# A two-layer decoder trunk on one core: gate and up projections of four small experts with separate high and low activations, and another order of the experts

## The chip, the cores and the metric

The kernel runs on one core of a Trainium2 chip. The metric is the time of one execution on the device, in microseconds (us). TensorE multiplies matrices and loads their stationary operand, VectorE (DVE), ScalarE (ACT) and GpSimd (POOL) compute elementwise, and SyncE (SP) issues the transfers of the weights.

## The reference

A sequence of 256 tokens of width 1024 goes through two layers. Layer 0 has two groups of attention heads and a dense SwiGLU. Layer 1 has stick-breaking attention and then a mixture of eight SwiGLU experts, of which the router picks two for each token. The change is in that last part:

```
def moe_swiglu(h, w_router, w_gate, w_up, w_down):
    logits = h @ w_router
    top_v, top_i = top_k(logits, 2)
    gates = sum(one_hot(top_i, 8) * softmax(top_v)[..., None])
    for e in range(8):
        y = y + gates[..., e] * ((silu(h @ w_gate[e]) * (h @ w_up[e])) @ w_down[e])
```

All numbers are float32. An expert has a gate and an up matrix of 1024 x 3584 and a down matrix of 3584 x 1024, 44 MB together, and the eight have 352 MB of the 432 MB that the kernel reads.

## The kernel before, in words

**Units.** All weights come in pieces of 128 partitions x 2048 float32 (1 MB), called units, in one fixed stream. An expert is 42 units: 14 of gate, 14 of up and 14 of down. SP (line 678) puts each into a ring of six raw slots as soon as the subtraction that used the slot six units earlier is done. The order inside an expert is written out by `moe_plan` (line 109): its 3584 hidden columns are cut into a chunk of 512 and three of 1024, and the units run gate 0 (2 units), up 0 (2), gate 1 (4), up 1 (4), down 0 (2), gate 2, up 2, down 1 (4 each), gate 3, up 3, down 2, down 3 (4 each).

**High and low parts.** The matmuls of the weights run in float32r, and the kernel splits every operand into two such parts: ACT copies a raw unit into a float32r tile `hi` (line 790, `split`), DVE subtracts it from the raw unit and writes the rest as `lo` (line 1286). Both rings have four slots in the expert stage (`HM`), and ACT fills a slot only when TensorE has used the unit four back. In program order ACT runs three units and DVE two units ahead of the step at which their other work stands (`used(k)`). The product of two split operands is made by `three` (lines 2003 to 2005): high by high, high activation by low weight, low activation by high weight, 512 columns each.

**Experts by load.** After the router, DVE sorts experts 1 to 7 by the number of their tokens (`order_experts`, line 1778). Expert 0 comes first. The four with the fewest tokens are "small" and have at most 64 tokens, or the kernel takes its other branch, which isn't taken here. The three others are "large" and have up to 128 rows. The eight places are numbered e = 0 to 7. In the kernel before, `SMALL` is [1, 3, 5, 7] and `LARGE` is [2, 4, 6], so they alternate.

**A large expert (and expert 0).** The token rows, gathered by an indirect transfer, are transposed on TensorE (`gather`, line 2467) and split into `xg_hi` and `xg_lo`. For each gate and up unit TensorE makes four groups of `three`, that is 12 matmuls (`columns`, line 2498). ACT applies Silu to the gate sums (`silu`, line 1089), DVE multiplies them with the up sums (`multiply`, line 1755), TensorE transposes the hidden activations in seven blocks of 512 columns (`g_transpose_h`, line 2560), ACT and DVE split each block (lines 1126 and 1798), and the down units take 12 matmuls each (`down`, line 2529).

**A small expert.** The 64 rows of high and the 64 rows of low activations stand side by side as one stationary operand of 128 columns, and `both` (line 2493) multiplies it by the high and by the low weights: eight matmuls for a unit, in gate, up and down. Rows 0 to 63 of the sum are then the high part's share and rows 64 to 127 the low part's. Silu isn't linear, so the two halves must be added before it. That is `turn` (line 2563): ACT copies the gate sums and the up sums out (`keep_gate`, line 1098, `keep_up`, line 1106), TensorE multiplies them by `fold64` (two identity matrices of 64 below each other) in float32, which transposes and adds the halves in one step. Then ACT applies Silu to a block of 128 x 256 (`turned_silu`, line 1114), DVE multiplies (`turned_multiply`, line 1761), and ACT and DVE split into high and low again (`turned_high`, line 1119, `turned_low`, line 1767). There are seven turns in an expert. The down sums are linear: both halves are stored and added on their way to memory (lines 766 and 768).

**Between experts.** ACT copies the down sums to SBUF (`y_copy`, line 1079), which marks the end of an expert in the trace. While expert e runs, DVE makes the table of the next one's tokens (line 1690), TensorE and DVE turn it into row numbers (lines 2592 and 1739), POOL gathers the rows (line 761). In expert 1 DVE computes where each token's results lie (`slot_numbers`, line 1715). In expert 7 POOL gathers those results (line 774) and DVE adds them (`add_result`, line 1745).

Of the kernel before, what the change touches and what calls it, by code (L numbers as in the profile page):

```python
# [29 lines left out]
P = 128  # L30
SEQ = 256
# [42 lines left out]
SMALL = [1, 3, 5, 7]  # L74
LARGE = [2, 4, 6]
# [67 lines left out]
def build(nc, x_d, rel_bias, ev_norm_mix, ev_w_in, ev_kv_norm, ev_w_uk, ev_w_uv, ev_cmp_pos, ev_cmp_w1,  # L143
# [93 lines left out]
    with ExitStack() as ctx:  # L237
# [96 lines left out]
        fold64 = after_layer0("fold64", [P, HALF])  # L334
# [50 lines left out]
        swish, h_turned = (probT[:, t].rearrange("p h q -> p (h q)").rearrange("p (s n) -> p s n", s=2) for t in range(T))  # L385
# [102 lines left out]
        t_silu_done = sem("t_silu_done")  # L488
        t_h_done = sem("t_h_done")
# [151 lines left out]
        def small_subs(e, s):  # L641

            return NSUB * len([i for i in SMALL if i < e]) + s

        def sub_slot(s):

            return s % 2
# [131 lines left out]
        def _(act):  # L779
# [283 lines left out]
            def gathered_high(e):  # L1063

                for b in range(2):
                    act.wait_ge(gathered, 2 * e + b + 1)
                    if e in SMALL:
                        act.activation(xg_hi[:, 4 * b:4 * b + 4, 0:HALF], ps[:, 4 + b, 0:SEQ].rearrange(
                            "p (k s) -> p k s", k=4), ACT.Copy).then_inc(xg_hi_ready, 1)
                        continue  # L1070
                    act.activation(xg_hi[:, 4 * b:4 * b + 4, :], ps[:, 4 + b, :].rearrange("p (k s) -> p k s", k=4),
                                   ACT.Copy).then_inc(xg_hi_ready, 1)
# [8 lines left out]
            def silu(e, c):  # L1081
# [7 lines left out]
                act.activation(work[:, 0, 0:w], ps[:, 4:4 + w // W, :].rearrange("p a n -> p (a n)"), ACT.Silu)\  # L1089
                    .then_inc(g_silu_done, 1)  # L1090

            def keep_gate(e, c):

                w = MOE_CHUNKS[c][1]
                act.wait_ge(units_used, first_of(e) + UP_AT[c])
                act.wait_ge(g_h_done, NCH * e + c)
                act.wait_ge(g_hT_done, NSUB * e + SUBS[c][0])
                act.activation(work[:, 0, 0:w], ps[:, 4:4 + w // W, :].rearrange("p a n -> p (a n)"), ACT.Copy)\  # L1098
                    .then_inc(g_silu_done, 1)

            def keep_up(e, c):

                w = MOE_CHUNKS[c][1]
                act.wait_ge(units_used, first_of(e) + UP_AT[c] + KD * w // UNIT)
                act.wait_ge(g_hT_done, NSUB * e + SUBS[c][0])
                act.activation(work[:, 1, 0:w], ps[:, 2:2 + w // W, :].rearrange("p a n -> p (a n)"), ACT.Copy)\
                    .then_inc(g_h_done, 1)

            def turned_silu(e, s):

                act.wait_ge(g_hT_done, NSUB * e + s + 1)
                if small_subs(e, s) >= 2:
                    act.wait_ge(t_h_done, small_subs(e, s) - 1)
                act.activation(swish[:, sub_slot(s)], ps[:, 7, 0:SEQ], ACT.Silu).then_inc(t_silu_done, 1)

            def turned_high(e, s):

                act.wait_ge(t_h_done, small_subs(e, s) + 1)
                act.activation(hT_both(s)[:, :, 0:HALF],
                               h_turned[:, sub_slot(s)].rearrange("p (j q) -> p j q", q=HALF), ACT.Copy)\  # L1120
                    .then_inc(g_hT_hi_ready, 1)
# [16 lines left out]
            with act.If(fits):  # L1138
                done[0] = U_MOE + HM
                gathered_high(0)  # L1140
                for e in range(NE):
# [7 lines left out]
                    if e in SMALL:  # L1149
                        used(UP_AT[0])  # L1150
                        keep_gate(e, 0)
                        used(GATE_AT[1])
                        keep_up(e, 0)
                        used(GATE_AT[1] + 2)
                        turned_silu(e, 0)
                        used(GATE_AT[1] + 3)
                        turned_high(e, 0)
                        used(UP_AT[1])
                        keep_gate(e, 1)
                        used(DOWN_AT[0])  # L1160
                        keep_up(e, 1)
                        used(GATE_AT[2])
                        if e == NE - 1:
                            act.wait_ge(placeT_done, 1)
                            act.activation(placeT[:], ps[:, 6, 0:SEQ], ACT.Copy).then_inc(placeT_ready, 1)
                        used(GATE_AT[2] + 2)
                        turned_silu(e, 1)
                        used(GATE_AT[2] + 3)
                        turned_high(e, 1)
                        used(UP_AT[2])  # L1170
                        turned_silu(e, 2)
                        keep_gate(e, 2)
                        used(UP_AT[2] + 1)
                        turned_high(e, 2)
                        used(DOWN_AT[1])
# [1577 lines left out]
```

## Time and profile before

| | |
|---|---|
| median of 3 runs | 1433.79 us (1429.02 to 1434.1) |
| the profiled execution | 1420.63 us, span 1418.8 us |
| mean granted TensorE clock | 0.986 |
| TensorE busy | 1369.0 us, 96% of the span |
| VectorE busy | 1097.6 us, 77% |
| ScalarE busy | 940.6 us, 66% |
| read from memory | 432.20 MB, mean 310 GB/s |
| expert stage (eight experts) | about 464 to 1407 us of the span |

Times of single rows are of the profiled execution. A matmul's duration in a row holds the time until its end has drained; the next one starts earlier, so the distance between two starts is what a matmul costs in a row of them. A row of a stretch gives its bounds, its length, each engine's busy time with its instructions, the granted clock (1.00 is full speed), the share of the DMA engines' time, and GB/s. "Idle before, with releaser" is the time an engine stood still ahead of the instruction, and what ended it.

### The profile page before, as it was taken

What the parts mean: (1) busy time and instruction counts of PE and PEld (TensorE: products, weight loads), DVE (VectorE), ACT (ScalarE), POOL (GpSimd) and SP (SyncE); (2) the same over time, 40 slices, a digit from 0 to 9 for tenths busy, and PEclk for the clock granted to TensorE, in tenths of its full rate; (3) what the DMA queues carried; (4) which work ended last, traced back from release to release, by engine and by line L of the source; (5) the groups of instructions that cost most, each with busy time, mean ns of one, the idle gap of its engine ahead of it and who ended that gap; (6) DMA issues with size and microseconds to landing.
All of it is one profiled execution on the core that took longest, in us unless ns stands there. A gap on an engine that the chain in (4) does not pass through costs nothing.

```text
span 1418.8 us, 16608 instructions
## 1 busy us (share of the span) xinstructions
PE 1369.0 (96%) x6550; PEld 1143.2 (81%) x6550; DVE 1097.6 (77%) x871; ACT 940.6 (66%) x767; POOL 49.3 (3%) x51
## 2 busy tenths in 40 slices
PE   8999999999999999999999999999999999999887
PEld 7886788887988788877888878878887878888766
DVE  4786644556465988888898898798898889888796
ACT  3565534335455677777777788687777777777764
POOL 0000000000010000000000000000000000002000
PEclk9999999999999999999999999999999999999998
DMA  9744455555632899999999999999999989999993
GB/s 311 214 159 149 155 205 178 178 179 177 224 119 92 334 373 382 379 387 399 322 407 390 364 400 407 393 366 398 379 374 414 408 324 397 394 368 392 412 360 115
DMA packets 136643, 439.13 MB, mean 310 GB/s; under 512 B 11520, under 2 KB 28912, under 8 KB 120816
## 3 DMA queue, kind: packets, MB, share of 16 engines
q1 hardware_dynamic: 130688, 424.24, 80.0%
q0 software_dynamic: 3392, 12.07, 2.5%
q10 hardware_dynamic: 2480, 1.69, 0.4%
q8 instruction: 54, 0.88, 0.3%
q14 instruction: 29, 0.24, 0.0%
HBM read 432.20 MB, written 5.78 MB: 309 GB/s over the span
## 4 chain that ended last, share of the span: by engine, by line
PE 73%; DVE 17%; ACT 5%; DMA 3%; issue 3%; ACTq 0%; SPq 0%; DVEq 0%
PE ps L2003 18%; PE ps L2005 18%; PE ps L2004 18%; DVE lo L1286 12%; PE ps L2575 7%; PE ps L2495 4%; PE ps L2496 4%; ACT hi L790 2%; DMA raw<-in_od_w_gate_dram 2%; PE ps L2560 1%; DMA wr<-in_od_w_router_dram 1%; ACT work L1098 1%; DVE work L1312 0%; PE ps L2299 0%; DMA x<-in_x_dram 0%
## 5 line engine op out<-in xcount | busy, mean ns | idle before, releaser
L1286 DVE TENSOR_TENSOR lo<-raw,hi 128x2048 fp32r<-128x2048 f32 (+1 forms) x403 | 904.9, 2285 | 102.9 <-ACT hi L790 101.2
L790 ACT ACTIVATE hi<-raw 128x2048 fp32r<-128x2048 f32 (+1 forms) x403 | 766.8, 1914 | 206.4 <-PE ps L2005 157.0
L2003 PE MATMUL ps<-hi,xT_hi 128*128 128x512 f32 (+1 forms) x752 | 294.6, 392 | 7.2 <-DVE lo L1286 4.6
L2005 PE MATMUL ps<-hi,xT_lo 128*128 128x512 f32 (+1 forms) x752 | 290.0, 386 | 0.0
L2004 PE MATMUL ps<-lo,xT_hi 128*128 128x512 f32 (+1 forms) x752 | 289.7, 385 | 0.0
L2495 PE MATMUL ps<-hi,xT_hi 128*128 128x512 f32 x448 | 187.4, 418 | 12.0 <-DVE lo L1286 11.0
L2496 PE MATMUL ps<-lo,xT_hi 128*128 128x512 f32 x448 | 181.4, 405 | 0.0
L2003 PEld LDWEIGHTS ps<-hi,xT_hi 128*128 128x128 f32 x752 | 141.7, 188 | 38.3 <-issue 5.5
L2005 PEld LDWEIGHTS ps<-hi,xT_lo 128*128 128x128 f32 x752 | 141.4, 188 | 28.7
L2004 PEld LDWEIGHTS ps<-lo,xT_hi 128*128 128x128 f32 x752 | 141.6, 188 | 26.4
L2495 PEld LDWEIGHTS ps<-hi,xT_hi 128*128 128x128 f32 x448 | 88.5, 198 | 45.5 <-DVE lo L1286 19.9
L2003 PE MATMUL ps<-hi,hT_hi 128*128 128x512 f32 x296 | 116.2, 393 | 0.0
L2005 PE MATMUL ps<-hi,hT_lo 128*128 128x512 f32 x296 | 115.4, 390 | 0.0
L2004 PE MATMUL ps<-lo,hT_hi 128*128 128x512 f32 x296 | 115.3, 390 | 0.0
L2575 PEld LDWEIGHTS ps<-fold,work 128*128 128x128 f32 x448 | 106.6, 327 | 1.1
L2575 PE MATMUL ps<-fold,work 128*128 128x64 f32 x448 | 104.3, 387 | 0.0
L2496 PEld LDWEIGHTS ps<-lo,xT_hi 128*128 128x128 f32 x448 | 88.1, 197 | 17.3
L2003 PE MATMUL ps<-xT_hi,hi 128*128 128x256 f32 (+1 forms) x256 | 73.0, 285 | 1.0 <-DVE lo L1286 1.0
L2004 PE MATMUL ps<-xT_lo,hi 128*128 128x256 f32 (+1 forms) x256 | 72.4, 283 | 0.0
L2005 PE MATMUL ps<-xT_hi,lo 128*128 128x256 f32 (+1 forms) x256 | 72.4, 283 | 0.0
L2005 PEld LDWEIGHTS ps<-hi,hT_lo 128*128 128x128 f32 x296 | 55.6, 188 | 11.6
L2003 PEld LDWEIGHTS ps<-hi,hT_hi 128*128 128x128 f32 x296 | 55.7, 188 | 11.1
(327 smaller groups left out, 1223.9 us busy)
## 6 DMA issues: line engine op xcount, KB each, us to landing
raw<-in_od_w_gate_dram SPq DMA_DIRECT2D x112, 1024.0 KB, 8.4
raw<-in_od_w_up_dram SPq DMA_DIRECT2D x112, 1024.0 KB, 9.4
raw<-in_od_w_down_dram SPq DMA_DIRECT2D x112, 1024.0 KB, 8.3
raw<-in_od_w_qkv_dram SPq DMA_DIRECT2D x12, 1024.0 KB, 5.2
raw<-in_ev_w_gate_dram SPq DMA_DIRECT2D x11, 1024.0 KB, 5.2
raw<-in_ev_w_up_dram SPq DMA_DIRECT2D x11, 1024.0 KB, 5.1
raw<-in_ev_w_down_dram SPq DMA_DIRECT2D x11, 1024.0 KB, 5.1
raw<-in_ev_w_in_dram SPq DMA_DIRECT2D x4, 1024.0 KB, 11.1
```

What stands on the lines that cost most here:

```text
L790: act.activation(unit(hi, n), unit(raw, n), ACT.Copy).then_inc(hi_ready, 1)
L1098: act.activation(work[:, 0, 0:w], ps[:, 4:4 + w // W, :].rearrange("p a n -> p (a n)"), ACT.Copy)\
L1286: dve.tensor_tensor(unit(lo, n), unit(raw, n), unit(hi, n).bitcast(F32), ALU.subtract)\
L2003: pe.matmul(out, s_hi, m_hi, start=start, stop=False, skip_group_check=True)
L2004: pe.matmul(out, s_hi, m_lo, start=False, stop=False, skip_group_check=True)
L2005: return pe.matmul(out, s_lo, m_hi, start=False, stop=stop, skip_group_check=True)
L2495: pe.matmul(out, s_both, m_hi, start=start, stop=False, skip_group_check=True)
L2496: return pe.matmul(out, s_both, m_lo, start=False, stop=stop, skip_group_check=True)
L2560: ins = pe.transpose(ps[:, 7, P * j:P * j + P], work[:, 1, f + j:f + W:4], ident[:])
L2575: ins = pe.matmul(ps[:, 7, first:first + HALF], work[:, part, f + j:f + W:4], fold64[:], start=True, stop=True)
```

## The change

For small experts only the down projection keeps the joined operand (`both`). Gate and up take `three` with a stationary operand of 64 columns, and write to rows 0 to 63. Silu, multiplication and transpose then go as in a large expert, on 64 rows. `turn`, its copies, its buffers and `fold64` are gone, and each engine runs one order of steps for all experts. The places change too: expert 0, the three largest, then the four small ones.

```diff
-SMALL = [1, 3, 5, 7]
-LARGE = [2, 4, 6]
+SMALL = [4, 5, 6, 7]
+LARGE = [1, 2, 3]
...
+        def rows_of(e):
+
+            return HALF if e in SMALL else P
...
-            def keep_gate(e, c):
...
-            def keep_up(e, c):
...
-            def turned_silu(e, s):
...
-            def turned_high(e, s):
...
+                n = rows_of(e)
+                act.activation(work[0:n, 0, 0:w], ps[0:n, 4:4 + w // W, :].rearrange("p a n -> p (a n)"), ACT.Silu)\
                     .then_inc(g_silu_done, 1)
...
             def g_hT_high(e, s):
 
                 act.wait_ge(g_hT_done, NSUB * e + s + 1)
+                if e in SMALL:
+                    act.activation(hT_both(s)[:, :, 0:HALF], ps[:, 7, 0:SEQ].rearrange("p (j q) -> p j q", q=HALF),
+                                   ACT.Copy).then_inc(g_hT_hi_ready, 1)
+                    return
...
-            def turned_multiply(e, s):
...
-            def turned_low(e, s):
...
+                n = rows_of(e)
+                dve.tensor_tensor(work[0:n, 1, 0:w], work[0:n, 0, 0:w],
+                                  ps[0:n, 2:2 + w // W, :].rearrange("p a n -> p (a n)"), ALU.mult).then_inc(g_h_done, 1)
...
             def g_hT_low(e, s):
 
                 dve.wait_ge(g_hT_hi_ready, NSUB * e + s + 1)
+                if e in SMALL:
+                    dve.tensor_tensor(hT_both(s)[:, :, HALF:P], ps[:, 7, 0:SEQ].rearrange("p (j q) -> p j q", q=HALF),
+                                      hT_both(s)[:, :, 0:HALF].bitcast(F32), ALU.subtract).then_inc(g_hT_ready, 1)
+                    return
...
-                        if e in SMALL:
-                            ins = both(ps[:, bank + m, :], xg_hi[:, k, :], wh[:, kk, cols], wl[:, kk, cols], k == 0,
-                                       k == KD - 1)
-                            continue
-                        ins = three(ps[:, bank + m, :], xg_hi[:, k, :], xg_lo[:, k, :], wh[:, kk, cols],
-                                    wl[:, kk, cols], k == 0, k == KD - 1)
+                        ins = three(ps[0:tokens, bank + m, :], xg_hi[:, k, 0:tokens], xg_lo[:, k, 0:tokens],
+                                    wh[:, kk, cols], wl[:, kk, cols], k == 0, k == KD - 1)
...
+                n = rows_of(e)
                 for j in range(4):
-                    ins = pe.transpose(ps[:, 7, P * j:P * j + P], work[:, 1, f + j:f + W:4], ident[:])
-                ins.then_inc(g_hT_done, 1)
-
-            def turn(e, s, c):
...
+                    ins = pe.transpose(ps[:, 7, n * j:n * j + n], work[0:n, 1, f + j:f + W:4], ident[0:n, 0:n])
                 ins.then_inc(g_hT_done, 1)
```

`gather`, `gathered_high` and `gathered_low` get the same `rows_of(e)`, and `order_experts` writes the sorted experts in one run each instead of every second place. The separate lists of steps for small experts on TensorE, ACT and DVE are taken out.

## Rows read from the trace of the kernel before

**Rows 1.** The page's first part: busy time of each engine, share of the span, instructions.

```profile
PE 1369.0 (96%) x6550; PEld 1143.2 (81%) x6550; DVE 1097.6 (77%) x871; ACT 940.6 (66%) x767; POOL 49.3 (3%) x51
```

**Rows 2.** Timeline of ACT (start, duration us): the y copy behind expert 1, of seven.

```profile
700.79 1.03 ACT L1079 ACTIVATE work<-ps 128x1024 f32<-128x1024 f32 x1 [0.18 <-PE ps L2496]
```

**Rows 3.** Stretches, experts 1, 2, 3, 5, 7: us; busy PE, PEld, DVE, ACT, POOL; clock; DMA.

```profile
583.30:700.80 117.50, 112.75 (x461) 91.68 (x459) 100.16 (x82) 90.59 (x68) 3.35 (x2) 0.96 0.98 377
700.80:820.30 119.50, 119.39 (x545) 99.30 (x546) 106.21 (x60) 88.81 (x56) 4.24 (x3) 1.00 1.01 382
820.30:932.80 112.50, 109.50 (x460) 89.42 (x459) 97.14 (x61) 90.78 (x67) 3.38 (x2) 0.98 1.00 394
...
1052.40:1167.60 115.20, 112.40 (x460) 91.50 (x458) 97.34 (x61) 91.06 (x68) 3.38 (x2) 0.96 0.98 384
...
1287.10:1407.30 120.20, 110.33 (x450) 90.67 (x448) 99.07 (x59) 86.64 (x66) 9.32 (x5) 0.96 0.87 338
```

**Rows 4.** Timeline of TensorE: a turn in small expert 1.

```profile
685.57 0.40 PE L2496 MATMUL ps<-lo,hT_hi 128*128 128x512 f32 x1
685.81 3.72 PE L2575 MATMUL ps<-fold,work 128*128 128x64 f32 x16
689.34 0.47 PE L2495 MATMUL ps<-hi,hT_hi 128*128 128x512 f32 x1
```

**Rows 5.** Timeline of TensorE: end of large expert 4, then a 64-row transpose.

```profile
1039.49 0.39 PE L2004 MATMUL ps<-lo,hT_hi 128*128 128x512 f32 x1
1039.72 0.39 PE L2005 MATMUL ps<-hi,hT_lo 128*128 128x512 f32 x1
1040.04 0.71 PE L2458 MATMUL ps<-ident,work 64*128 64x64 f32 x8
```

**Rows 6.** Groups by line, small expert 3 (820.3 to 932.8): busy us, mean ns, idle before.

```profile
L1098 ACT ACTIVATE work<-ps 128x1024 f32<-128x1024 f32 (+1 forms) x4 | 3.6, 911 | 0.0
L1106 ACT ACTIVATE work<-ps 128x1024 f32<-128x1024 f32 (+1 forms) x4 | 3.6, 908 | 0.0
L1761 DVE TENSOR_TENSOR probT<-probT,ps 128x256 f32<-128x256 f32 x7 | 3.0, 421 | 13.0 <-ACT probT L1114 13.0
L1114 ACT ACTIVATE probT<-ps 128x256 f32<-128x256 f32 x7 | 2.7, 383 | 14.6 <-PE ps L2575 14.6
```

**Rows 7.** Groups by line, large expert 4 (932.8 to 1052.4).

```profile
L1755 DVE TENSOR_TENSOR work<-work,ps 128x1024 f32<-128x1024 f32 (+1 forms) x4 | 4.3, 1087 | 2.3 <-PE ps L2005 2.3
L1089 ACT ACTIVATE work<-ps 128x1024 f32<-128x1024 f32 (+1 forms) x4 | 3.7, 920 | 1.8 <-PE ps L2005 1.8
```

**Rows 8.** A stretch inside small expert 3, columns as in rows 3.

```profile
829.40:910.00 80.60, 78.37 (x325) 63.71 (x324) 70.48 (x44) 64.72 (x48) 2.80 (x1) 0.98 1.02 409
```

**Rows 9.** Timeline of ACT in small expert 3: splits that waited for their unit.

```profile
855.54 1.92 ACT L790 ACTIVATE hi<-raw 128x2048 fp32r<-128x2048 f32 x1 [0.63 <-DMA raw<-in_od_w_gate_dram]
858.11 1.91 ACT L790 ACTIVATE hi<-raw 128x2048 fp32r<-128x2048 f32 x1 [0.65 <-DMA raw<-in_od_w_up_dram]
```

**Rows 10.** Stretches at half clock: the first and last of ten.

```profile
598.40:601.80 3.40, 3.40 (x9) 2.72 (x10) 2.67 (x3) 2.49 (x3) 0.00 (x0) 0.50 1.05 423
1397.10:1400.60 3.50, 3.50 (x10) 2.74 (x9) 3.50 (x4) 3.04 (x3) 0.00 (x0) 0.51 0.00 0
```

**Rows 11.** Timelines of DVE and ACT in large expert 2: the down stage.

```profile
753.43 8.89 DVE L1286 TENSOR_TENSOR lo<-raw,hi 128x2048 fp32r<-128x2048 f32 x4
...
763.02 1.22 DVE L1755 TENSOR_TENSOR work<-work,ps 128x1024 f32<-128x1024 f32 x1 [0.70 <-PE ps L2005]
...
791.31 1.92 ACT L790 ACTIVATE hi<-raw 128x2048 fp32r<-128x2048 f32 x1 [0.80 <-PE ps L2005]
```

**Rows 12.** Timeline of DVE in expert 1: first and last of the slot numbers.

```profile
604.21 0.58 DVE L1719 TENSOR_SCALAR rslot<-splace 128x2 f32<-128x2 f32 x7
...
607.67 0.17 DVE L1732 CAST rslot_id<-rslot_at 128x4 uint32<-128x4 f32 x1
```

**Rows 13.** Group by line in the last expert (1287.1 to 1407.3).

```profile
L1745 DVE SCALAR_TENSOR_TENSOR x<-results,rslot_gate,x 128x1024 f32<-128x1024 f32 x4 | 5.1, 1278 | 0.0
```

More of the change, by code:

```diff
@@ L1778, in order_experts @@
             def order_experts():
-                for first, count, at_load in ((0, len(SMALL), len(LARGE)), (1, len(LARGE), 0)):
-                    ins = dve.tensor_tensor(stands_at[:, first:NE - 1:2, :],
+                for first, count, at_load in ((0, len(LARGE), 0), (len(LARGE), len(SMALL), len(LARGE))):
+                    ins = dve.tensor_tensor(stands_at[:, first:first + count, :],
                                             by_load[:, at_load:at_load + count].unsqueeze(2)
@@ L2452, in gather @@
             def gather(e):
-                if e in SMALL:
-                    pe.wait_ge(rows_landed, 16 * e)
-                    pe.wait_ge(g_silu_done, NCH * e)
-                    for k in range(KD):
-                        ins = pe.transpose(ps[:, 4 + k // 4, HALF * (k % 4):HALF * (k % 4) + HALF], rows[0:HALF, P * k:P * k + P],
-                                           ident[0:HALF, 0:HALF])
-                        if k % 4 == 3:
-                            ins.then_inc(gathered, 1)
-                    return
                 if e:
@@ L2465, in gather @@
                     pe.wait_ge(g_silu_done, NCH * e)
+                    n = rows_of(e)
                     for k in range(KD):
-                        ins = pe.transpose(ps[:, 4 + k // 4, P * (k % 4):P * (k % 4) + P], rows[:, P * k:P * k + P], ident[:])
+                        ins = pe.transpose(ps[:, 4 + k // 4, n * (k % 4):n * (k % 4) + n], rows[0:n, P * k:P * k + P],
+                                           ident[0:n, 0:n])
                         if k % 4 == 3:
@@ L2500, in columns @@
                 n = first_of(e) + base + q
+                tokens = rows_of(e)
                 w = MOE_CHUNKS[c][1]
@@ L2558, in g_transpose_h @@
                 f = W * (s - SUBS[c][0])
+                n = rows_of(e)
                 for j in range(4):
-                    ins = pe.transpose(ps[:, 7, P * j:P * j + P], work[:, 1, f + j:f + W:4], ident[:])
-                ins.then_inc(g_hT_done, 1)
-            def turn(e, s, c):
-                pe.wait_ge(g_silu_done, NCH * e + c + 1)
-                pe.wait_ge(g_h_done, NCH * e + c + 1)
-                if s:
-                    pe.wait_ge(t_h_done, small_subs(e, s))
-                else:
-                    pe.wait_ge(g_hT_ready, NSUB * e)
-                f = W * (s - SUBS[c][0])
-                for part in range(2):
-                    for j in range(4):
-                        first = SEQ * part + HALF * j
-                        ins = pe.matmul(ps[:, 7, first:first + HALF], work[:, part, f + j:f + W:4], fold64[:],
-                                        start=True, stop=True)
+                    ins = pe.transpose(ps[:, 7, n * j:n * j + n], work[0:n, 1, f + j:f + W:4], ident[0:n, 0:n])
                 ins.then_inc(g_hT_done, 1)
```

183 lines of the change are left out of this document (5 added, 178 removed).

## The prediction

> **What bounds the kernel now.** I read the page's busy times first [rows 1]: TensorE is busy in 96% of the span, but a matmul's row includes its drain, so this isn't yet 96% of its rate. Then I cut the expert stage at the y copies, one behind each expert [rows 2], and read each piece [rows 3]. All large experts take 119.5 us and TensorE is busy for 119.4 of it: they are bound by TensorE. The small ones take 117.5, 112.5, 115.2 and 120.2 us (sum 465.4), though they have a third fewer matmuls in a unit. TensorE stands still there for 3 to 10 us, DVE is busy for 97 to 100 us and ACT for 87 to 91, and the clock is 0.96 to 0.98 where the large ones have 1.00. So what does a small expert wait for?
>
> Two matmuls of 512 columns start 0.23 us apart [rows 5]; 504 of them in a large expert make 114.5 us at 0.227. A unit of 12 matmuls is 2.73 us, a unit of eight 1.82. DVE subtracts one unit every 2.22 us (four in 8.89) [rows 11] and ACT copies one in 1.91 [rows 9]. A unit arrives every 2.56 us: two ACT splits that both waited for their transfer start 2.57 us apart [rows 9], and over 80 us the DMA engines are full at 409 GB/s [rows 8], where 1.0486 MB take 2.56 us. So between turns a small expert's TensorE could go at 1.82 us a unit but gets one every 2.2 to 2.6. At a turn, TensorE alone works for 3.5 us, 685.81 to 689.34 [rows 4], while the slots fill up and ACT waits for it (14.6 us in seven turns) and DVE for ACT (13.0 us) [rows 6]. The work is uneven: TensorE is too fast in one step and too slow in the next. And the clock is at its lower level, 1.2 GHz, in ten stretches of 3.4 us [rows 10], all of them in small experts, during a turn or right behind one; no large expert has any.
>
> **TensorE's work.** Removed per small expert: seven turns of 3.55 us, 24.9 us. Added: one matmul for each of 28 units x 4 groups, 112 x 0.227 = 25.4 us, and seven blocks of four transposes. Eight 64-row transposes show 0.71 us [rows 5], so 28 take 2.5. The sum is +3 us: TensorE gets more to do, not less. Counted from below: 28 x 2.73 + 14 x 1.82 = 101.9; a large expert's other work (transposes, gather, row numbers) is 119.5 - 114.5 = 5.0, and with 64 rows I take 4.0 (bounds 3 and 5). That is 106 us, against some 103 before.
>
> The trace has no float32r matmul with 64 stationary columns and 512 moving ones. By the rows at hand its cost is 0.227 us, since the moving columns are the same; a loaded array of half the columns could save nothing in a row that streams 512. Bounds: 0.21 and 0.25 us, which is -6 or +8 us per expert. I take 0.227.
>
> **DVE.** Out go seven multiplications of 0.42 us (3.0 us [rows 6]); in come four larger ones, 4.3 us [rows 7], if 64 partitions take as long as 128 (lower bound half, 2.2). The subtraction stays at 128 x 256. 97.1 - 3.0 + 4.3 = 98.4 us busy.
>
> **ACT.** Out go the two copies (3.6 + 3.6) and Silu in blocks (2.7) [rows 6]; in comes Silu on 64 rows, 3.7 [rows 7]. 90.8 - 6.2 = 84.6 us. Neither engine's sum is the bound; the turn's chain TensorE, ACT, DVE, ACT, DVE gets shorter by two links, and its waits of 13 us on DVE mostly go.
>
> **What is late next: the down units.** Gate and up now run at TensorE's 2.73 us a unit, slower than DVE (2.22) and DMA (2.56). But a down unit is 1.82 us, and there DVE is late. Walked for down 1 (four units, t = 0 where TensorE begins them): the copy of a unit starts when TensorE has used the one four back, as the ACT row's wait on TensorE says [rows 11]. Two down units are ready at t = 0. DVE's multiplication needs the last up unit and takes 1.22, then come 2.2 per unit: the third down unit is ready at 3.4, the fourth at 5.6, the next gate unit at 7.8. TensorE wants them at 3.6, 5.5 and 7.3. It loses 0.6 us. For down 2 and 3 (eight units in a row) the same walk has DVE need 1.2 + 6 x 2.2 + 1.6 (two blocks' low parts and the gathered rows), about 16.3 beyond t = 0, where TensorE needs 14.5 + 1.6 of transposes and gather, and the ordering behind transposes adds some 2: it loses 2.2. Down 0 has two units and loses nothing. So TensorE with its waits takes 106 + 2.8 = 108.8 us.
>
> **DMA.** An expert moves 44.04 MB of weights, 0.26 MB of gathered rows and 0.52 MB of stored results: 44.8 MB, at 409 GB/s [rows 8] 109.6 us. At the mean rate of all of expert 3, 394 GB/s [rows 3], it is 113.7. These are the bounds; I take 111, nearer to the saturated stretch. So DMA becomes the bound by about 2 us. The first of the four small experts follows a large one, whose pace of 2.73 us a unit lets the six raw slots fill, so 110 for it, then 111, 111.
>
> The last one also gathers 2.1 MB of results (5.1 us of DMA) and adds them in 5.1 us of DVE, among the down units [rows 13]; part of each shows, 5 in all: 116. Together 448 against 465.4: -17.4. The seven turns' half clock, at most 1.7 us for each of ten stretches [rows 10], is inside these numbers and not counted twice.
>
> **The moved step.** With the new order expert 1 is large, and the slot numbers (604.21 to 607.84, 3.6 us of DVE [rows 12]) fall into it. A large expert's DVE is ahead of TensorE by about one unit and idle 13 us in all, so most of it is hidden; bounds 0 and 3.6, I take +1.0. The gather, stores and place tables keep their place inside an expert. Four small experts in a row instead of alternating costs only that DMA can't catch up between them, which is priced above. At the end, the same steps follow the last down unit.
>
> Sum: -17.4 + 1.0 = -16.4 us. The profiled execution goes from 1420.63 us (span 1418.8 and 1.8 around it) to 1404; the median of the runs shown is 13 us higher, 1433.79, and I carry the difference over: 1417.
>
> **Two rules of the Trainium skill.** In rows 5 the 64-column transpose starts 0.32 us behind a 128-column matmul instead of 0.23, 0.09 more. TensorEngine Tiling (Array Packing), Key Properties, says that a change of the tiling mode drains TensorE; if 64 columns count as another mode, some 16 changes in a small expert at 0.16 us, the drain that a 0.39 us row shows beyond its 0.23 us distance, would be 2.6 us each, about 10 in all (rival 4). The trace so far shows a smaller price.
>
> Rows 8 show 409 GB/s. DMA: Bandwidth & Descriptors, Where 436 GB/s comes from, says that memory, at about 358 GB/s per core, limits loads to SBUF; by that a small expert would need 125 us and the change could win nothing. The trace, with one core at work, is above it, and the measurement decides.
>
> **The rivals.**
> 1. TensorE sets the pace (108.8) because the full raw slots carry DMA through: 4 x 109 + 4 = 440, -24.4 with the moved step, 1409. For it: large experts end with loaded slots. Against: three small ones follow one another. Chance 0.13 (1403 to 1411).
> 2. DMA keeps expert 3's mean of 394 GB/s: 113.7 x 3 + 118 = 459, -5.4, 1428. For it: that row has a DMA share of 1.00. Against: that time holds hiccups of the turns. Chance 0.20 (1424 to 1431).
> 3. Slower: nothing is saved up for the down units. Gate and up take 76.4 + 4.0 as their full price, and the down units wait for DVE and the hidden blocks, 2.8 us each instead of 1.82. Then a small expert is 119.6, the last 124: 483, +18.4 with the moved step, 1452. It decides from about 2.47 us per down unit on, where the sum is that of before. For it: a ring of four slots and ACT copies bound to TensorE's step four units back [rows 11]. Against: in a large expert DVE waits 13 us, so it stands ahead. Chance 0.09.
> 4. The change of array width costs 10 us: 1427. Chance 0.03. That a half-used array falls to the lower clock for long would cost 70 us per expert; the trace has the lower level only around turns, and I give it under 0.01.
>
> **Numbers.** The forecast's own case (1411 to 1424) has 0.55. About 0.5% (7 us) can be told from no change. Faster by more than that, under 1426.6: 0.55 + 0.13 + 0.08 of rival 2, 0.76. Within: the rest of rival 2 and rival 4, 0.15. Slower: 0.09. The range 1406 to 1431 leaves out a part of rival 1 and rival 3.
>
> **What would show it.** Small experts at 110 to 112 us each (y copy to y copy), the last near 116; large ones still 119.5, expert 1 about 120.5. TensorE busy nearly all of a small expert, matmuls of 64 columns 0.227 us apart, ACT splits there waiting for their transfer and no longer for turns, no half clock. The prediction is wrong if down units take over 2.4 us, if 64-column matmuls are slower than 0.23 us, or if DVE's waits for ACT stay at 13 us.

## The result, and the profile after

The changed kernel takes 1408.31 us (median of 4 runs, 1406.98 to 1412.28), the kernel before beside it 1431.4 us (4 runs, 1424.79 to 1434.1). The ratio is 0.985, with a 95% interval of 0.9808 to 0.9892: 23 us faster, well beyond the 7 us that can be told from no change. The forecast was 1417 (1406 to 1431).

The profiled execution took 1406.98 us against 1420.63, only 13.7 less. That the medians stand 23 us apart and the profiled executions 13.7 matters below.

The page's first part, after (answers to [rows 1]):

```profile
PE 1368.6 (97%) x6662; PEld 1059.4 (75%) x6662; DVE 1103.2 (79%) x858; ACT 925.2 (66%) x723; POOL 47.1 (3%) x51
```

TensorE has 112 more matmuls, DVE and ACT have fewer instructions, and none of these sums says where 13.7 us went. The stretches do. Cut where the last down matmul of each expert ends (after it comes the y copy, up to 0.6 us later), after (answers to [rows 3]; columns: bounds, length, busy us and count of PE, PEld, DVE, ACT, POOL, then clock, DMA share, GB/s; the first row is expert 0, then come the large experts 1 to 3 and the four small ones):

```profile
463.10:583.80 120.70, 118.39 (x534) 98.46 (x534) 107.77 (x67) 87.54 (x55) 2.81 (x1) 0.99 0.96 358
583.80:703.80 120.00, 119.38 (x545) 99.16 (x545) 106.65 (x80) 89.02 (x56) 3.36 (x2) 1.00 0.99 379
703.80:823.00 119.20, 119.20 (x546) 99.36 (x545) 104.02 (x59) 89.03 (x56) 3.33 (x2) 1.00 1.00 378
823.00:942.10 119.10, 119.10 (x545) 98.84 (x545) 103.71 (x59) 88.71 (x56) 3.31 (x2) 1.00 0.99 374
942.10:1053.60 111.50, 110.67 (x488) 69.64 (x486) 98.40 (x58) 86.00 (x56) 3.29 (x2) 1.00 1.01 392
1053.60:1165.40 111.80, 110.80 (x488) 69.84 (x488) 101.08 (x59) 87.00 (x57) 4.22 (x3) 1.00 1.02 403
...
1277.20:1393.70 116.50, 110.70 (x479) 69.01 (x478) 103.29 (x58) 83.02 (x55) 8.10 (x6) 1.00 0.91 361
```

The small experts take 111.5, 111.8, 111.8 (the row left out) and 116.5, together 451.6 against 465.4: 13.8 us less. The large ones take 358.3 against 358.6. Expert 0, where the clock fell once to 1.2 GHz, is 1.7 us longer than before, and what lies outside the experts makes up for most of that. TensorE is busy for 110.8 of 111.8 us, and the clock is 1.00 in all seven other pieces. DMA is nearly full too (403 GB/s).

Who waits for whom in the second small expert (idle time by engine and releaser: us in total, times, longest):

```profile
ACT hi L782 <- PE ps L1860: 10.6, 13, 0.9
ACT hi L782 <- DMA raw<-in_od_w_up_dram: 6.1, 7, 1.8
...
DVE work L1664 <- PE ps L1860: 4.0, 4, 1.2
DVE hT_hi L1694 <- ACT hT_hi L1086: 3.5, 2, 1.7
PEld ps L2406 <- issue: 2.4, 6, 0.4
DVE hT_lo L1694 <- ACT hT_lo L1086: 2.0, 2, 1.6
```

DVE waited 13.0 us for ACT in the seven turns of a small expert before [rows 6]; now it waits 5.5 for ACT at the hidden blocks, and 4.0 for TensorE before its multiplications. ACT's splits wait for TensorE (10.6) and for transfers (6.1 and 4.3 for the up and gate weights) about equally. And TensorE's load of the transposes (L2406) stands still for 0.4 us before each of six blocks, with nothing in the profile that holds it back.

What the new instructions cost, same expert (columns: operation, shapes, count, busy us, mean ns, idle time before):

```profile
L1858 PE MATMUL ps<-hi,xT_hi 128*64 128x512 f32 x112 | 44.1, 394 | 0.4 <-DVE lo L1199 0.4
...
L2406 PE MATMUL ps<-ident,work 64*128 64x64 f32 x28 | 4.8, 291 | 0.0
L2406 PEld LDWEIGHTS ps<-ident,work 64*128 64x128 f32 x28 | 3.9, 210 | 2.4 <-issue 2.4
L1664 DVE TENSOR_TENSOR work<-work,ps 64x1024 f32<-64x1024 f32 x3 | 3.6, 1213 | 3.6 <-PE ps L1860 3.6
L1079 ACT ACTIVATE work<-ps 64x1024 f32<-64x1024 f32 x3 | 3.1, 1018 | 1.9 <-PE ps L1860 1.9
```

The multiplication and Silu on 64 partitions take 1.21 and 1.02 us, what they take on 128 (1.22 in [rows 11] and 1.03 in the trace before).

The idle time of TensorE in such rows is too low. A matmul's row holds its drain, so a short wait hides behind it. Here a down unit came late, its first matmul starts 0.42 us behind the last one instead of 0.23, and no idle time is marked:

```profile
1120.94 0.39 PE L2344 MATMUL ps<-lo,hT_lo 128*128 128x512 f32 x1
1121.36 0.50 PE L2343 MATMUL ps<-hi,hT_lo 128*128 128x512 f32 x1
```

Taken from the distances between starts, TensorE waits about 2.5 us in this expert, nearly all of it at down units; the marked idle time is 1.1.

### The profile page after: what moved, and what is told of

Read it like the earlier page. It is cut to its first block, busy times and chain, and to the rows that moved or that the text cites. A ratio compares the mean times of both kernels' runs of the same rounds, so it can differ in the third digit from the quotient of the medians.

```text
span 1405.2 us, 16748 instructions
## 1 busy us (share of the span) xinstructions
PE 1368.6 (97%) x6662; PEld 1059.4 (75%) x6662; DVE 1103.2 (79%) x858; ACT 925.2 (66%) x723; POOL 47.1 (3%) x51
## 4 chain that ended last, share of the span: by engine, by line
PE 80%; DVE 14%; ACT 3%; DMA 2%; issue 2%; ACTq 0%; SPq 0%; DVEq 0%
PE ps L1858 25%; PE ps L1860 24%; PE ps L1859 24%; DVE lo L1199 8%; PE ps L2406 2%; DMA raw<-in_od_w_down_dram 1%; ACT hi L782 1%; DMA wr<-in_od_w_router_dram 1%; DVE work L1664 1%; PE ps L2343 1%; PE ps L2344 1%; DVE work L1225 0%; PE ps L2154 0%; DMA x<-in_x_dram 0%; PE ps L2049 0%
## 5 line engine op out<-in xcount | busy, mean ns | idle before, releaser
L1858 PE MATMUL ps<-hi,xT_hi 128*128 128x512 f32 (+2 forms) x1200 | 471.2, 393 | 11.5 <-DVE lo L1199 8.9
L1860 PE MATMUL ps<-hi,xT_lo 128*128 128x512 f32 (+2 forms) x1200 | 466.3, 389 | 0.0
L1859 PE MATMUL ps<-lo,xT_hi 128*128 128x512 f32 (+2 forms) x1200 | 465.9, 388 | 0.0
L1858 PEld LDWEIGHTS ps<-hi,xT_hi 128*128 128x128 f32 (+1 forms) x1200 | 202.0, 168 | 87.8 <-issue 11.4
L1860 PEld LDWEIGHTS ps<-hi,xT_lo 128*128 128x128 f32 (+1 forms) x1200 | 201.9, 168 | 71.4
L1859 PEld LDWEIGHTS ps<-lo,xT_hi 128*128 128x128 f32 (+1 forms) x1200 | 202.0, 168 | 66.8
L1858 PE MATMUL ps<-hi,hT_hi 128*128 128x512 f32 x296 | 116.1, 392 | 0.0
L1859 PE MATMUL ps<-lo,hT_hi 128*128 128x512 f32 x296 | 115.2, 389 | 0.0
L1859 PEld LDWEIGHTS ps<-lo,hT_hi 128*128 128x128 f32 x296 | 55.6, 188 | 11.2
L2343 PE MATMUL ps<-hi,hT_hi 128*128 128x512 f32 x128 | 51.1, 399 | 0.7 <-DVE lo L1199 0.7
L2344 PE MATMUL ps<-lo,hT_hi 128*128 128x512 f32 x128 | 50.0, 391 | 0.0
L1858 PEld LDWEIGHTS ps<-xT_hi,hi 128*128 128x128 f32 (+1 forms) x256 | 48.2, 188 | 1.6 <-DVE lo L1199 1.2
```

What stands on the lines that cost most here:

```text
L1858: pe.matmul(out, s_hi, m_hi, start=start, stop=False, skip_group_check=True)
L1859: pe.matmul(out, s_hi, m_lo, start=False, stop=False, skip_group_check=True)
L1860: return pe.matmul(out, s_lo, m_hi, start=False, stop=stop, skip_group_check=True)
L2343: pe.matmul(out, s_both, m_hi, start=start, stop=False, skip_group_check=True)
L2344: return pe.matmul(out, s_both, m_lo, start=False, stop=stop, skip_group_check=True)
```

## The experiments

Three theories stood against each other. A: the turn's chain over three engines was what a small expert waited for, and taking it away is the gain. B: the gain is the clock, since the stretches at 1.2 GHz [rows 10] all stood at turns. C: the new order of the experts brings part of it. The later runs ask what bounds the kernel after, and what would make it faster still.

**E1: the new order alone**, in the kernel before.

```diff
-SMALL = [1, 3, 5, 7]
-LARGE = [2, 4, 6]
+SMALL = [4, 5, 6, 7]
+LARGE = [1, 2, 3]
```

> The kernel before with the new order of the experts alone (SMALL 4 to 7, LARGE 1 to 3, the sorted experts written in two runs); small experts keep joined gate and up and their turns. Theory (the gain is from the small experts' own work: no turns, an even pace on TensorE, no half clock): no gain from the order; small experts 112 to 118 us each, the last about 120, half-clock stretches in them as before, time within 0.4% of before. Rival (order matters, since alternating makes the transfers start and stop): a third or more of the 1.5% gain, 7 us or more. Other rival (four small ones in a row starve on transfers): 5 us slower or more.

Measured: 1433.88 us (10 runs), ratio 1.0027 (1.0007 to 1.0047). The order brings nothing; if anything it costs a few us. The last small expert takes 126.2 us where about 120 was expected. Three of its four small experts (the third takes 118.1), stretches as above:

```profile
943.20:1057.80 114.60, 112.27 (x461) 90.98 (x459) 96.89 (x61) 90.02 (x67) 3.29 (x2) 0.96 0.99 383
1057.80:1175.70 117.90, 114.71 (x461) 92.50 (x460) 99.81 (x63) 90.80 (x68) 4.22 (x3) 0.94 0.99 381
...
1293.80:1420.00 126.20, 112.96 (x451) 90.44 (x450) 101.69 (x61) 86.70 (x67) 8.85 (x6) 0.96 0.86 329
```

**E2: the new gate and up projections alone**, in the alternating order.

```diff
-SMALL = [4, 5, 6, 7]
-LARGE = [1, 2, 3]
+SMALL = [1, 3, 5, 7]
+LARGE = [2, 4, 6]
```

> The changed kernel with the old alternating order of the experts (SMALL 1, 3, 5, 7). Theory: the whole gain stays, ratio 0.983 to 0.988, small experts 111 to 112 us each and the last near 116. Rival (order carries a part): ratio 0.990 or more.

Measured: 1408.23 us, ratio 0.9841 (0.9795 to 0.9886), the time of the changed kernel. Its small experts take 112.8, 112.0, 112.0 and 113.8 us; the last:

```profile
1281.90:1395.70 113.80, 110.00 (x479) 68.92 (x477) 100.49 (x56) 82.77 (x55) 11.09 (x5) 1.00 0.90 356
```

C falls: the whole gain is in the projections. In the alternating order the last small expert is 2.7 us shorter and the others 0.2 to 1.3 longer; these cancel.

**E3: longer chains at the same work.** In the kernel before, each turn is cut into two halves with a weight unit between them.

```diff
-                        turn(e, 0, 0)
-                        gate(e, 1, 2, 3)
+                        turn(e, 0, 0, (0,))
+                        gate(e, 1, 2)
+                        turn(e, 0, 0, (1,))
+                        gate(e, 1, 3)
```

> The kernel before with each turn cut in two halves of four matmuls (1.8 us each) with one unit's eight matmuls between them; same work, same order of the experts. Theory (half of the loss is that a turn of 3.5 us stops the supply of slots and brings half clock behind it): small experts 1 to 4 us shorter each, fewer half-clock stretches than ten, time 4 to 12 us lower. Rival (only the amount of work and the number of links of the chain count): no change within 0.3%, clock share as before. Third: the longer chain from first to second half delays ACT and DVE and it gets slower by 4 us or more.

Measured: 1444.79 us, ratio 1.0097 (1.0063 to 1.0131), though the clock rose to 0.993 to 0.997. The gain that the theory expected didn't come; the third case did, a longer chain that costs more than the clock gives back. The second small expert's waits and stretch:

```profile
ACT probT L1114 <- PE ps L2571: 25.4, 7, 4.3
DVE probT L1761 <- ACT probT L1114: 20.1, 7, 3.6
```

```profile
825.10:944.30 119.20, 109.44 (x461) 87.14 (x459) 97.05 (x61) 89.81 (x67) 3.37 (x2) 1.00 0.96 372
```

In the kernel before these waits are 14.6 and 13.0 [rows 6] in 112.5 us [rows 3]. DVE waits 7.1 us more and the expert gets 6.7 longer, with the same work on each engine (DVE 97.1 busy in both). This is A's mechanism, shown in the direction of longer waits: what the turn's chain keeps DVE waiting is not made up elsewhere, and sets a small expert's time. It is no evidence against B. In the experts one stretch at 1.2 GHz is left, from 611.2 us, and no half turn stands ahead of it but a wait of 3.62 us:

```profile
611.39 0.79 PE L2495 MATMUL ps<-hi,xT_hi 128*128 128x512 f32 x1 [3.62 <-DVE lo L1286]
```

**E4: the changed kernel once more**, unchanged, beside E1 to E3.

> The changed kernel once more, for comparison on the same chip: ratio 0.985 within its interval of 0.981 to 0.989, granted clock 0.996 or more. If the kernel before runs at 1424 to 1434 us unprofiled because of more half-clock stretches than in its trace, its clock share in these runs is below 0.986 whenever it is slower than 1421 us.

Measured: 1408.54 us, ratio 0.9848 (0.9804 to 0.9893). The gain stands. The runs of the kernel before in that comparison run from 1424.28 to 1437.59 us with granted clocks of 0.985 to 0.974. Over its 39 runs beside E1 to E11 time falls with the clock, by 1.1 us for each 0.001 (correlation -0.88). The profiled execution had 0.986, at the lucky end.

**E5: a wide fold.** In the kernel before, the turn's moving operand has 128 columns instead of 64 (the second half is a copy whose result is overwritten). A turn takes 3.32 us from its first to its last start, as before; no link of the chain is taken away (DVE waits for it 11.6 us in expert 3, against 13.0).

```diff
-        fold64 = after_layer0("fold64", [P, HALF])
+        fold64 = after_layer0("fold64", [P, P])
...
-                        ins = pe.matmul(ps[:, 7, first:first + HALF], work[:, part, f + j:f + W:4], fold64[:],
+                        n = HALF if first + HALF == W else P
+                        ins = pe.matmul(ps[:, 7, first:first + n], work[:, part, f + j:f + W:4], fold64[:, 0:n],
                                         start=True, stop=True)
```

> The kernel before; in each turn the moving operand has 128 columns instead of 64 (the fold matrix twice), and the next matmul overwrites the surplus half. The load of the strided float32 stationary operand (327 ns in the rows) should go on setting the pace, so a turn stays near 3.5 us, but TensorE streams twice as many columns in it. Theory (the gain of the change is mostly the half clock that follows the narrow turns; in runs before the clock share was 0.974 to 0.985, and the time went with it): clock share over 0.993, at most 3 half-clock stretches, median 12 to 20 us lower, nearly the changed kernel. Rival (the gain is the shorter chain behind a turn, for which DVE waits 13 us per expert): clock may rise but the time falls by less than 5 us; if a turn gets longer by x, DVE waits 7x more per expert and the time rises.

Measured: 1419.35 us (7 runs), ratio 0.993 (0.9904 to 0.9957): 11.4 us less than the 1430.8 of the kernel before beside it, just under the 12 that were expected, and well above the rival's 5. The clock is 0.991 to 0.995. Its stretches for experts 1, 3 and 5:

```profile
586.30:702.90 116.60, 110.34 (x460) 90.31 (x459) 100.13 (x82) 90.10 (x67) 3.36 (x2) 0.97 0.99 378
...
822.50:935.50 113.00, 108.90 (x460) 87.95 (x459) 97.49 (x61) 90.88 (x67) 3.37 (x2) 1.00 1.00 392
...
1055.10:1167.20 112.10, 108.92 (x460) 87.95 (x459) 97.06 (x61) 90.65 (x67) 3.38 (x2) 1.00 1.01 396
```

What TensorE did before the clock fell tells the two kernels apart. In the kernel before, each of the ten stretches begins at the end of a turn or right behind one. One of them, in expert 5, from 1124.1 us on (matmuls of 0.63 us instead of 0.39 are at 1.2 GHz):

```profile
1121.06 3.77 PE L2575 MATMUL ps<-fold,work 128*128 128x64 f32 x16
1124.58 0.78 PE L2495 MATMUL ps<-hi,xT_hi 128*128 128x512 f32 x1
1125.16 0.63 PE L2496 MATMUL ps<-lo,xT_hi 128*128 128x512 f32 x1
```

With the wide fold no stretch comes behind a turn. The small experts have two left, of 6.8 us each, and both come behind a wait of TensorE for DVE, of 3.62 us in expert 1 and of 1.96 in the last. The first:

```profile
613.03 0.80 PE L2496 MATMUL ps<-hi,xT_hi 128*128 128x512 f32 x1 [3.62 <-DVE lo L1286]
613.62 0.63 PE L2497 MATMUL ps<-lo,xT_hi 128*128 128x512 f32 x1
```

So B is about half of the gain; the interval of the ratio allows 6 to 14 us. This rests on the medians. The two profiled executions took nearly the same (1420.12 and 1420.63), and in them three stretches cost expert 5 3.1 us (115.2 against 112.1) and a single one cost expert 3 nothing (112.5 against 113.0). E1's second small expert, at 0.94, took 117.9; part of that can be its place behind another small expert.

**E6: 128-row transposes.** In the changed kernel, small experts transpose all 128 rows and ACT and DVE read the 64 columns that count.

```diff
-                    ins = pe.transpose(ps[:, 7, n * j:n * j + n], work[0:n, 1, f + j:f + W:4], ident[0:n, 0:n])
+                    ins = pe.transpose(ps[:, 7, P * j:P * j + P], work[:, 1, f + j:f + W:4], ident[:])
```

> The changed kernel; the transposes of a small expert's hidden blocks run over all 128 rows and give 128 columns (the upper 64 are left over from earlier and not read). In the changed kernel a block of four 64-row transposes lengthens its unit by 0.77 us, in a large expert by 0.51. Theory (TensorE bounds a small expert at 110.8 us busy of 111.8, and 64-row transposes cost a change of shape): 0.51 a block, 1.8 us less per small expert, 4 to 7 us in all. Rival (transfers bound it, 42 units at 2.6 us and the stores): under 2 us in all.

Measured: 1405.45 us (6 runs), ratio to before 0.9841 (0.9812 to 0.9871). Small experts 110.0, 110.4, 110.3 and 117.8: 1.4 to 1.5 us less in each of the first three, and the last 1.3 longer. The median is 2.9 us below the changed kernel's, between the rival's 2 and the 4 to 7 that were expected.

**E7: nothing narrow on TensorE.** As E6, and gate and up of small experts load 128 stationary columns, half of them without meaning.

```diff
-                tokens = rows_of(e)
+                tokens = P
```

> As the wide transposes, and also gate, up and the gather of small experts with 128 stationary columns and rows (the upper 64 left over, their sums not read). No TensorE instruction of the expert stage has 64 rows or columns any more; the number of matmuls is the same. Theory (TensorE-bound): a unit 2.73 instead of 2.76 us, 28 of them 0.9 us, with the transposes 2.7 us per small expert, limited by the transfers near 109.6: 6 to 10 us in all. Rival (transfer-bound): under 3 us. Third (128 columns are dearer to load, 188 instead of 134 ns): no gain over the wide transposes.

Measured: 1403.52 us (6 runs, 1402.69 to 1405.58), ratio 0.9826 (0.9797 to 0.9855). Small experts 109.2, 109.7, 110.7, 118.6. More columns, less time: 4.8 us below the changed kernel, though 6 to 10 were expected; in part that is the last expert, which got 2.1 us longer. A block of four transposes on TensorE's timeline (start, duration), first in the changed kernel, then in this one:

```profile
1128.96 0.40 PE L1860 MATMUL ps<-hi,xT_lo 128*64 128x512 f32 x1
1129.29 0.69 PE L2406 MATMUL ps<-ident,work 64*128 64x64 f32 x4
1129.91 0.45 PE L1858 MATMUL ps<-hi,xT_hi 128*64 128x512 f32 x1
1130.20 0.39 PE L1859 MATMUL ps<-lo,xT_hi 128*64 128x512 f32 x1
```

```profile
1125.07 0.39 PE L1860 MATMUL ps<-hi,xT_lo 128*128 128x512 f32 x1
1125.30 0.63 PE L2405 MATMUL ps<-ident,work 128*128 128x128 f32 x4
1125.69 0.48 PE L1858 MATMUL ps<-hi,xT_hi 128*128 128x512 f32 x1
1126.01 0.39 PE L1859 MATMUL ps<-lo,xT_hi 128*128 128x512 f32 x1
```

From the first start to the last it is 1.24 us against 0.94. Two distances of 0.23 taken off, the narrow block costs 0.78 us and the wide one 0.48. The difference is 0.3 us a block, about 2 us in the seven blocks of an expert. The Trainium skill's rule (TensorEngine Tiling (Array Packing), Key Properties) that a change of the tiling mode drains TensorE fits the 64-row block, though no run isolates a drain. The 64 columns of the gate and up matmuls have no part in it: in E6, where they stay, a wide block costs what it costs here, and in the changed kernel a 128-column matmul starts its usual 0.23 us behind a 64-column one:

```profile
1087.42 0.39 PE L1860 MATMUL ps<-hi,xT_lo 128*64 128x512 f32 x1
1087.65 0.40 PE L2343 MATMUL ps<-hi,hT_hi 128*128 128x512 f32 x1
```

**E8: the transfers' floor.** The changed kernel without the third product (low activation by high weight) in gate and up of small experts. That part of the result is left out.

```diff
+                        if e in SMALL:
+                            ins = both(ps[0:tokens, bank + m, :], xg_hi[:, k, 0:tokens], wh[:, kk, cols],
+                                       wl[:, kk, cols], k == 0, k == KD - 1)
+                            continue
```

> The changed kernel without the third product (low activation by high weight) in gate and up of small experts: that part of the product is left out. TensorE has 112 matmuls of 0.23 us less per small expert, 25.7 us. Theory (TensorE, transfers and DVE lie within 2 us of each other): small experts fall only to the transfers' or DVE's pace, 108 to 110.5 us, 5 to 14 us in all. If TensorE alone bounded them with nothing near, they would fall below 100.

Measured: 1401.02 us (4 runs), ratio 0.98 (0.9762 to 0.9838). Third small expert:

```profile
1157.50:1267.90 110.40, 91.59 (x376) 52.71 (x376) 101.79 (x59) 86.21 (x57) 4.20 (x3) 1.00 1.03 405
```

TensorE has 19 us less to do, and the expert is only 1.4 us shorter than in the changed kernel. The DMA share is 1.03 at 405 GB/s, and ACT's splits wait there for transfers, 24.7 us in all, so I read 110.4 us as what the transfers allow once the raw slots are used up. No run takes away the third product and half of the transfers together, so this bound is argued and not shown. The first small expert, which finds full raw slots, went below it (105.3). Its clock fell as well, without any turn: three stretches of 3.4 us in its small experts, each behind a wait of TensorE for DVE of 1.83 to 2.36 us:

```profile
1074.05 0.41 PE L2343 MATMUL ps<-hi,xT_hi 128*64 128x512 f32 x1 [2.36 <-DVE lo L1199]
...
1075.00 0.63 PE L2344 MATMUL ps<-lo,xT_hi 128*64 128x512 f32 x1
```

**E9: E7 in the alternating order**, with the two lists of E2.

> The wide kernel (no TensorE instruction of 64 columns or rows in small experts) with the alternating order of before. If the order only decides how the raw slots stand when the last expert's extra 2.1 MB of gathered results come, then behind a large expert the slots are full: the last small expert takes 113 to 114 us instead of 118.6, the others 110 to 111, and the sum is 1399 to 1401. Rival: the order is worth nothing here either, since what the last one wins the others lose: 1403 to 1405.

Measured: 1401.5 us (6 runs, 1398.24 to 1402.49), ratio 0.98 (0.9776 to 0.9825). First, second and last small expert:

```profile
586.60:697.40 110.80, 108.29 (x488) 87.78 (x486) 101.55 (x78) 86.83 (x56) 3.35 (x2) 1.00 1.00 392
...
817.00:926.80 109.80, 108.09 (x489) 87.92 (x487) 98.89 (x58) 86.74 (x56) 3.37 (x2) 1.00 1.01 400
...
1275.70:1388.40 112.70, 108.08 (x479) 86.81 (x477) 100.56 (x56) 82.80 (x55) 10.61 (x5) 1.00 0.91 362
```

The small experts take 443.1 us against E7's 448.2: the last one, behind a large expert, takes 112.7 instead of 118.6, even less than the 113 to 114 that were expected, and the median is half a microsecond above its range of 1399 to 1401. The difference of 2.0 between the medians can't be told from none (the two intervals overlap). It is the fastest complete version that was run.

**E10: half the transfers.** E7, with only the first half of each unit loaded in small experts. The other half of the weights is left out, and all engines work as in E7.

```diff
-                    sp.dma_start(unit3(raw, n), src).then_inc(raw_landed[n % R], 16)
+                    part = shape_of(n)[0] // (2 if e in SMALL else 1)
+                    sp.dma_start(unit3(raw, n)[:, 0:part], src[:, 0:part]).then_inc(raw_landed[n % R], 16)
```

> The wide kernel whose small experts load only the first half of each 1 MB unit (the rest of a slot keeps old weights; everything else is computed as before). This leaves out half of their transfers, so its time is that of the engines alone. If the transfers are the floor of the wide kernel (110.4 us per small expert) with TensorE close behind, a small expert takes 107 to 109 us and the last one 111 to 113: 1389 to 1397. Rival: the engines' own chain (TensorE 109.2 to 110.7) is already the bound and only the last expert gets shorter: 109 to 110.5 each, 1396 to 1400.

Measured: 1396.82 us (4 runs), ratio 0.977 (0.9739 to 0.9801). Third and last small expert:

```profile
1162.30:1272.00 109.70, 108.39 (x488) 88.15 (x488) 100.97 (x60) 86.49 (x56) 4.21 (x3) 1.00 0.69 210
1272.00:1384.30 112.30, 108.18 (x479) 87.12 (x478) 102.88 (x58) 82.65 (x55) 10.34 (x6) 1.00 0.61 195
```

At half the bytes the third takes 109.7 us (E7: 110.7), the second the same 109.7 as in E7. The median lies in both ranges, but the stretches speak for the rival: with TensorE's 109.7 as the bound, only the last expert gets much shorter. TensorE's 109.7 and the 110.4 read off E8 are 0.7 apart in the wide kernel. Only the last one, with the 2.1 MB of gathered results on top, was held by transfers: 118.6 to 112.3.

**E11: the slot numbers moved**, in E5's kernel, from the small expert 1 to the large expert 2.

```diff
-                        if e == 1:
-                            slot_numbers()
...
-                    if e == 1:
+                    if e == 2:
```

> The kernel before with the turn's moving operand 128 columns wide, and with DVE's slot numbers (3.6 us) moved from a small expert to a large one. If DVE is the pacing engine of a small expert and has slack in a large one, expert 1 gets 3 to 3.6 us shorter (116.6 to about 113), the large one at most 1 us longer: 1416 to 1417 against 1419.35. Rival: the slot numbers were hidden in the small expert too, or cost as much in the large one: 1419.

Measured: 1416.96 us (6 runs), ratio 0.9916 (0.989 to 0.9942), inside the range that was expected; E5 had 0.993. Experts 1, 2 and 7:

```profile
584.90:697.00 112.10, 108.89 (x460) 87.92 (x459) 97.08 (x61) 90.77 (x67) 3.35 (x2) 1.00 1.01 396
697.00:817.50 120.50, 119.70 (x545) 99.16 (x546) 109.03 (x82) 88.80 (x56) 4.24 (x3) 1.00 1.00 381
...
1281.40:1400.90 119.50, 107.86 (x450) 86.94 (x449) 99.17 (x59) 86.41 (x66) 6.28 (x5) 1.00 0.87 339
```

Expert 1 falls from 116.6 to 112.1, more than the 3.6 us moved: the wait of 3.62 us in E5 is gone, and with it the 6.8 us at 1.2 GHz behind it. Expert 2 grows by 0.9. Where DVE paces, its extra work costs at least its own length; where TensorE does, a quarter of it. The medians (2.4 us apart, with overlapping intervals) don't settle it; the stretches do.

**Where the shorter chain pays.** E11 and E2 have the same order and a clock of 1.00 in these pieces, one with turns and one without. Their small experts take 112.1, 112.7, 112.1 and 119.5 us with turns, and 112.8, 112.0, 112.0 and 113.8 without. The two in the middle gain 0.1 and 0.7 us, although DVE's waits for ACT at the hidden activations fell from 13.0 us to 5.2. The last one gains 5.7, and expert 1 carries the 3.6 us of slot numbers without turns and is only 0.7 longer. So the waits that went away bring little by themselves. DVE now waits for TensorE instead (4.4 us before its multiplications), which sets the pace, and extra work fits into that. The time comes back where DVE has extra work: 3.6 us in expert 1, and, as I read it without a run that moves them, the 5.1 us of adding the results in the last [rows 13].

## Why the prediction was right

**The sum.** The small experts were forecast at 448 from 465.4 and came out at 451.6; the moved step at +1.0, and expert 1 is 0.8 to 0.9 us longer than the two other large ones. The profiled execution was to be 1404 and was 1407.

**What paced a small expert before.** "The turn's chain gets shorter by two links, and its waits of 13 us on DVE mostly go": they fell to 5.5, and E3 shows that longer waits reach the time almost one to one. Shorter ones don't, because TensorE (111.8) and the transfers (110.4) stand right behind.

**TensorE's work, mis-sized.** The step "28 x 2.73 + 14 x 1.82 = 101.9" plus "other work" of 4.0 and 2.8 of waits gave 108.8; TensorE's pace is 111.8. A gate or up unit takes 2.76 us instead of 2.73, 0.8 in an expert. The waits for DVE are about 2.5 us by the distances between starts, against 2.8 in the walk. The other work is some 6 us instead of 4.0, and this is the term that was too small: the seven blocks of narrow transposes cost 0.78 us each, 5.5 together. Eight in a row [rows 5] had given 2.5 for all of them. A block of four pays for its entry (0.33 us instead of 0.23) and its 0.62 us as often as it comes; eight in a row, in the gather, take 0.55 from the first to what follows.

**Which engine is the bound.** "DMA becomes the bound by about 2 us" failed: TensorE is, by 1.4 us if E8's 110.4 is the transfers' own time (111 was forecast). E6 and E7 take TensorE's excess away, and then both stand within 0.7 (E10). So rival 1, TensorE's pace, is the case that holds, at 111.8 instead of 108.8. That its time of 1409 is the one nearest to the measurement is luck, since its experts were to take 109. Rival 2's rate of 394 GB/s didn't stay; the second and third small expert have 403.

**The half clock, the largest miss.** I wrote that the turns' half clock "is inside these numbers and not counted twice", and then: "the median of the runs shown is 13 us higher, and I carry the difference over". But that difference was for the most part the half clock itself, which strikes more often in most executions than in the profiled one (clock 0.974 to 0.987 over 39 runs, with a median of 0.981, against 0.986), and the change takes it away: the changed kernel's median is 1.3 us above its profile. The terms: E5, 11.4 us for the stretches behind turns; E11 against E5, 2.4 for the slot numbers and the stretch behind them; the changed kernel against E11, 8.7 for the shorter chain and the slack that it gives DVE. Together 22.5 of the 23. Two errors of opposite sign, 3 us too much in the profile and 12 too little in what lies beyond it, left the forecast 9 us high, inside its range. That they partly cancelled is luck. The terms come from runs beside different runs of before, so each is sure to a few us only.

**The rivals that fell.** Rival 3 (slower): a down unit would have had to take 2.47 us; with its waits it takes about 2.0. Rival 4 (drains at 16 changes of width, 10 us): at a change from 64 to 128 stationary columns the starts stay 0.23 us apart, and the 64-row transposes cost about 2 us per expert.

**Still open.** That narrow turns are followed by 1.2 GHz and wide ones of the same length are not is what the profiles before, of E5 and of E11 show (E11 has none in its experts); why is not shown. Turns are not the only thing that the clock falls behind: waits of TensorE of 1.8 to 3.6 us stand ahead of the stretches that E3, E5 and E8 have left in their small experts. Why the last small expert grows from 116.5 to 118.6 as the others shrink is not separated either; E10 shows only that transfers hold it.

## What to carry to other kernels

When the median of a kernel lies well above its profiled execution and the granted clock varies from run to run, the difference is itself a cost with a place in the profile: ask whether the change touches that place before carrying it over. An engine that is busy for 85% of a stage can still pace it, if its waits on a chain of other engines can't be made up. The sum of its work and its waits doesn't show that, since it comes out at the stage's length for every engine; making the chain longer (E3) or moving some of its work (E11) does. Taking such waits away brings only as much as the next bound leaves, and pays most where the engine has extra work. To read how long TensorE waits, take the distances between starts and not the marked idle time. And fewer rows or columns on TensorE saved nothing here while the 512 moving columns stayed; transposes of 64 rows between wide matmuls were dearer than those of the full 128.

## What the runs showed that I had not expected

- All ten stretches at 1.2 GHz in the profile before began at the end of a turn of 64 moving columns or right behind it. With 128 columns in turns of the same 3.32 us, or with halved turns, none did, and the wide ones took 11.4 us off the median (E5, E3).
- The stretches at 1.2 GHz that were left in the small experts of E3, E5 and E8 (3.4 or 6.8 us long) came behind waits of TensorE of 1.8 to 3.6 us.
- Four 64-row transposes between matmuls cost 0.78 us, four of 128 rows 0.48 (E7). The first narrow one starts 0.33 us behind the matmul before it instead of 0.23, and the next matmul 0.62 us behind that instead of 0.39.
- Matmuls with 64 stationary columns pace a unit at 2.76 us, with 128 at 2.73, though their load takes 134 ns against 188. From a matmul with 64 to the next with 128 it is the usual 0.23 us.
- Silu and multiplication on 64 partitions take as long as on 128 (1.02 and 1.21 us for 1024 columns).
- One core at work moves 405 GB/s over a whole expert of 110.4 us (E8). The Trainium skill (DMA: Bandwidth & Descriptors, Where 436 GB/s comes from) states about 358 GB/s per core as memory's limit, half of a stack's rate; the measurement decides.
